# Holding four weight slots at each end of a product, with a ring of five raw and four high slots

## What is computed

```python
h = rmsnorm(x, g_pre_mix)
proj = h @ w_in                                   # 1024 x 3404: four attentions, 4 heads of 64 each
mix = concat(o_a, o_b, o_c, o_d)                  # sparse, forgetting, differential, sliding window
x = x + rmsnorm(mix @ w_out, g_post_mix)
h = rmsnorm(x, g_pre_mlp)
m = square(relu(h @ w_up)) @ w_down               # 4096 hidden
x = x + rmsnorm(m, g_post_mlp)
x = x + sigmoid(x @ w_ple_gate) * (p_i @ w_ple_proj)
```

## Time and profile before

| | |
|---|---|
| median of 3 runs | 2321.94 us (2321.07 to 2325.41) |
| the profiled execution: time | 2323.49 us |
| its span | 2321.5 us |
| mean granted TensorE clock | 0.942 |
| PE busy | 93% |
| DVE, ACT, POOL busy | 69%, 53%, 24% |
| read from HBM | 474 MB, 205 GB/s over the span |

### The profile page before, as it was taken

How to read it: one execution, slowest core, us unless ns; L and a number is a source line. 1 busy time by engine, 2 the same in 40 slices (tenths; PEclk the granted TensorE clock), 3 DMA queues, 4 the chain that set the end, 5 groups by cost and what they waited for, 6 DMA issues and landing times.

```text
span 2321.5 us, 28810 instructions
## 1 busy us (share of the span) xinstructions
PE 2150.0 (93%) x10728; PEld 1817.6 (78%) x10728; DVE 1600.0 (69%) x1615; ACT 1230.7 (53%) x1284; POOL 560.2 (24%) x355
## 2 busy tenths in 40 slices
PE   7978999898899989889998988799999999999995
PEld 5766888676778878777887877688888888888884
DVE  6675543577554358655345865698988989889896
ACT  4353443444454345443443544377777777777772
POOL 3413455332254533224554312000000000000000
PEclk9968999997799999899999989799999999999997
DMA  8403555442255544305554410499999999999993
GB/s 296 133 10 108 183 177 200 139 155 66 73 161 179 191 167 139 107 1 182 185 182 163 146 55 1 154 352 335 358 346 339 360 344 355 341 344 354 348 356 124
DMA packets 150508, 476.33 MB, mean 205 GB/s; under 512 B 12329, under 2 KB 39441, under 8 KB 150289
## 3 DMA queue, kind: packets, MB, share of 16 engines
q1 hardware_dynamic: 147792, 465.65, 56.9%
q0 software_dynamic: 2624, 9.44, 1.2%
HBM read 474.00 MB, written 1.05 MB: 205 GB/s over the span
## 4 chain that ended last, share of the span: by engine, by line
PE 78%; DVE 15%; ACT 3%; issue 2%; POOL 1%; DMA 0%; DVEq 0%; SPq 0%; POOLq 0%; ACTq 0%
PE G L581 19%; PE G L583 18%; PE G L582 18%; PE Sp L581 4%; PE Sp L583 4%; PE Sp L582 4%; PE G L607 3%; DVE ring_lo L1631 2%; PE Sp L744 2%; PE G L1136 1%; DVE ARENA L2074 1%; ACT ring_hi L1241 1%; PE G L1164 1%; PE G L1013 1%; PE Sp L1029 1%
## 5 line engine op out<-in xcount | busy, mean ns | idle before, releaser
L2307 DVE TENSOR_TENSOR e_lo<-e_raw,e_hi 128x1408 fp32r<-128x1408 f32 x384 | 600.8, 1619 | 27.0 <-ACT e_hi L1565 25.3
L1565 ACT ACTIVATE e_hi<-e_raw 128x1408 fp32r<-128x1408 f32 x384 | 520.7, 1380 | 159.1 <-DMA e_raw<-in_moe_w_down 55.9
L2407 POOL TENSOR_TENSOR ring_lo<-ring,ring_hi 128x640 fp32r<-128x640 f32 (+2 forms) x179 | 451.2, 2524 | 612.9 <-ACT ring_hi L1241 601.1
L1631 DVE TENSOR_TENSOR ring_lo<-ring,ring_hi 128x1408 fp32r<-128x1408 f32 (+2 forms) x179 | 320.6, 1799 | 292.1 <-ACT ring_hi L1241 291.0
L1241 ACT ACTIVATE ring_hi<-ring 128x2048 fp32r<-128x2048 f32 (+2 forms) x179 | 335.8, 1883 | 295.1 <-PE G L583 293.6
L581 PE MATMUL G<-ring_hi,xTh 128*128 128x512 f32 (+2 forms) x976 | 396.1, 406 | 36.6 <-DVE xTl L1647 30.6
L582 PE MATMUL G<-ring_lo,xTh 128*128 128x512 f32 (+2 forms) x976 | 387.3, 397 | 0.0
L583 PE MATMUL G<-ring_hi,xTl 128*128 128x512 f32 (+2 forms) x976 | 386.7, 396 | 0.0
L581 PE MATMUL G<-e_hi,xgTh 128*128 128x512 f32 (+1 forms) x768 | 290.0, 378 | 4.2 <-DVE e_lo L2307 4.2
L583 PE MATMUL G<-e_hi,xgTl 128*128 128x512 f32 (+1 forms) x768 | 289.1, 376 | 0.0
L582 PE MATMUL G<-e_lo,xgTh 128*128 128x512 f32 (+1 forms) x768 | 287.0, 374 | 0.0
(11 more groups left out here) (390 smaller groups left out, 3058.4 us busy)
## 6 DMA issues: line engine op xcount, KB each, us to landing
e_raw<-in_moe_w_gate SPq DMA_DIRECT2D x128, 704.0 KB, 5.9
e_raw<-in_moe_w_up SPq DMA_DIRECT2D x128, 704.0 KB, 5.9
e_raw<-in_moe_w_down SPq DMA_DIRECT2D x128, 704.0 KB, 5.9
ring<-in_w_in SPq DMA_DIRECT2D x48, 1024.0 KB, 5.1
ring<-in_w_mlp_up SPq DMA_DIRECT2D x32, 1024.0 KB, 5.3
ring<-in_w_mlp_down SPq DMA_DIRECT2D x32, 1024.0 KB, 4.8
ring<-in_w_out SPq DMA_DIRECT2D x16, 1024.0 KB, 4.9
ring<-in_ffn_w_gate SPq DMA_DIRECT2D x22, 512.0 KB, 3.8
```

Of the source, the lines that this page charges most:

```text
L1565: nc.scalar.activation(e_hi[:, u, :], e_raw[:, u, :], ACT.Copy).then_inc(w_hi.sem, 1)
L1631: v.tensor_tensor(ring_lo[:, n % R, cs], ring[:, n % R, cs], ring_hi[:, n % H, cs].bitcast(F32), ALU.subtract).then_inc(w_lo.sem, 1)
L2307: v.tensor_tensor(e_lo[:, u, :], e_raw[:, u, :], e_hi[:, u, :].bitcast(F32), ALU.subtract).then_inc(w_lo.sem, 1)
L2407: g.tensor_tensor(ring_lo[:, t % R, cs], ring[:, t % R, cs], ring_hi[:, t % H, cs].bitcast(F32), ALU.subtract).then_inc(w_lo_pool.sem, 1)
```

## The change

The ring becomes R = 5 raw and H = 4 high slots, in the same memory. Four slots are held at the end and at the start of products (`LEAD`): all of token block 0, then all of block 1.

- `product_rows` holds its last four slots. In block 1's last slot, after the first of its four groups, stands `tail()`: the transposes of block 0 for the next product.
- `lead` takes the place of `transposed_in`: block 0 through four slots, with the transposes of block 1 behind the first group of the fourth; then block 1 through four. Products over columns lead with two chunks (four slots, four banks), and wait for T0 and T1 and for their banks one by one. `product_tokens` is one lead with a tail. The first chunk of `w_in_2` keeps two slots (`first_chunk`).
- The low parts of 24 slots are made by DVE whole (`whole_dve`): the leading four of w_in in layer 1, of w_up twice, w_ple_proj and w_ple_gate twice (five each), and the first two of w_in_2.
- On ACT, DVE and POOL the parts of the next product's leading slots are put between the steps of the norms; before, only one stood ahead of them.

```diff
-R = 6
-H = 3
+R = 5
+H = 4
+LEAD = 4
...
+    whole_dve = []
     for l in range(DEPTH):
+        if l:
+            whole_dve += range(len(TILES), len(TILES) + LEAD)
         for n0, n1 in IN_CHUNKS:
             TILES += uses_cols(w["w_in"][l], n0, n1)
         TILES += uses_rows(w["w_out"][l])
+        whole_dve += range(len(TILES), len(TILES) + LEAD)
         for n0 in range(0, D_FF, 512):
             TILES += uses_cols(w["w_mlp_up"][l], n0, n0 + 512)
-        TILES += uses_rows(w["w_mlp_down"][l]) + uses_rows(w["w_ple_proj"][l]) + uses_rows(w["w_ple_gate"][l])
+        TILES += uses_rows(w["w_mlp_down"][l])
+        whole_dve += range(len(TILES), len(TILES) + 1 + LEAD)
+        TILES += uses_rows(w["w_ple_proj"][l]) + uses_rows(w["w_ple_gate"][l])
+    whole_dve += range(len(TILES), len(TILES) + 2)
...
-    def of_dve(m):
-
-        return m * 11 // 32 * 2
+    def of_dve(n):
+
+        m = floats_of(TILES[n])
+        return m if n in whole_dve else m * 11 // 32 * 2
+
+    def pool_parts(n):
+
+        return n - sum(t < n for t in whole_dve)
...
-            pe.wait_ge(w_lo_pool.sem, n + 1)
+            pe.wait_ge(w_lo_pool.sem, pool_parts(n + 1))
...
-        def transposed_in(src, ready, part, banks, between=None):
-
-
-            token_transposes(src, 0, ready)
-            if between:
-                between()
+        def lead(src, ready, part, banks_of, slots_per_half, tail, after_first=None):
+
+            slots = []
+            for j in range(LEAD):
+                if j == 0:
+                    bank_free_t(0)
+                if j == slots_per_half:
+                    bank_free_t(1)
+                banks_free(banks_of(j, 0))
+                slots.append(weights())
+                if j == LEAD - 1:
+                    part(slots[j], j, 0, range(1))
+                    token_transposes(src, 1, ready)
+                    last = part(slots[j], j, 0, range(1, 4))
+                else:
+                    last = part(slots[j], j, 0, range(4))
+                if j == 0 and after_first:
+                    after_first()
+            if slots_per_half == 2:
+                last.then_inc(g_half.sem, 1)
+            for j in range(LEAD):
+                if j == 0:
+                    bank_free_t(0)
+                if j == slots_per_half:
+                    bank_free_t(1)
+                banks_free(banks_of(j, 1))
+                if j == LEAD - 1 and tail:
+                    part(slots[j], j, 1, range(1))
+                    tail()
+                    last = part(slots[j], j, 1, range(1, 4))
+                else:
+                    last = part(slots[j], j, 1, range(4))
+                last.then_inc(w_used.sem, 1)
...
+        def first_cols(src, ready, widths, by):
+
+            lead(src, ready, lambda slots, j, tb, groups: cols_tile(slots, j % 2, tb, widths[j // 2], 2 * (j // 2) + tb, groups),
+                 lambda j, tb: [2 * (j // 2) + tb], 1, None)
+            for q in range(2):
+                chunk_made([2 * q, 2 * q + 1], by)
+
...
+        def product_rows(ah, al, n_tiles, by, behind, tail):
+
+
+            banks_free(range(4))
+            for t in range(n_tiles - LEAD):
...
-                for j in range(2):
+                for j in range(LEAD):
+                    k0 = 2 * (n_tiles - LEAD + j)
                     if tb == 0:
                         slots.append(weights())
-                    last = rows_tile(slots[j], 2, ah, al, 2 * (n_tiles - 2 + j), 2 * n_tiles, tb, g_of(tb))
+                    elif j == LEAD - 1:
+                        rows_tile(slots[j], 2, ah, al, k0, 2 * n_tiles, tb, g_of(tb), range(1))
+                        tail()
+                    last = rows_tile(slots[j], 2, ah, al, k0, 2 * n_tiles, tb, g_of(tb), range(1 if tb and j == LEAD - 1 else 0, 4))
                     if tb:
                         last.then_inc(w_used.sem, 1)
-                    elif j:
+                    elif j == LEAD - 1:
                         last.then_inc(g_half.sem, 1)
-            chunk_made(range(4), by, times)
-
-        def product_tokens(src, ready, by, between=None, times=1):
-
-            transposed_in(src, ready, lambda slots, j, tb: rows_tile(slots, 2, xTh, xTl, 2 * j, KT, tb, g_of(tb)), range(4), between)
-            product_rows(xTh, xTl, KT // 2, by, 2, times)
+            tokens_made(by)
...
+        def product_tokens(src, ready, by, tail, after_first=None):
+
+            lead(src, ready, lambda slots, j, tb, groups: rows_tile(slots, 2, xTh, xTl, 2 * j, KT, tb, g_of(tb), groups),
+                 lambda j, tb: [2 * tb, 2 * tb + 1], 2, tail, after_first)
+            tokens_made(by)
...
-            product_tokens(XN, o_block, ("dve",))
+            token_transposes(XN, 0, o_block)
+            product_tokens(XN, o_block, ("dve",), lambda: token_transposes(XN, 0, xn_block))
...
-            product_rows(hTh, hTl, 16, ("dve",), behind=(lambda: hidden(7), own_embedding))
+            product_rows(hTh, hTl, 16, ("dve",), (lambda: hidden(7), own_embedding), lambda: token_transposes(X, 0, x_block))
...
-            product_tokens(X, x_block, ("act",), embed_second, NTB)
+            product_tokens(X, x_block, ("act",), lambda: token_transposes(XN, 0, xn_block) if l + 1 < DEPTH else token_transposes(X, 0, x_block), embed_second)
...
-            first_cols(X, x_block, IN2_CHUNKS[0][1] - IN2_CHUNKS[0][0], [0, 1], ("act",))
+            first_chunk(X, x_block, IN2_CHUNKS[0][1] - IN2_CHUNKS[0][0], ("act",))
...
-            product_tokens(XN, xn_block, ("dve",))
+            token_transposes(XN, 0, xn_block)
+            product_tokens(XN, xn_block, ("dve",), lambda: token_transposes(X, 0, x_block))
...
         def normed_in(n, of_product):
 
 
-            met(n, 1)
+            met(n, 0)
             for tb in range(NTB):
                 of_product(tb)
-                if tb:
-                    block_evac(0)
+                met(0, 1 + 2 * tb)
                 mean_square_of_x(tb)
-            met(0)
-            block_evac(1)
+                met(0, 2 + 2 * tb)
+                block_evac(tb)
...
-            met(15, 1)
-            for tb in range(NTB):
-                mean_square_of_product(tb)
-            met(0)
-
-            met(1)
-            for tb in range(NTB):
-                if tb == 0:
-                    act.wait_ge(pe2a.sem, pe2a.next("act"))
-                else:
-                    act.wait_ge(w_used.sem, n_use["act"])
-                nc.scalar.activation(PLR[:, tb, :], Sp[:, :, :].rearrange("p b n -> p (b n)"), ACT.Copy).then_inc((a2d if tb else a2pe).sem, 1)
-                block_evac(tb)
+            met(15, 0)
+            mean_square_of_product(0)
+            met(0, 2)
+            block_evac(0)
+            met(0, 3)
+            mean_square_of_product(1)
+            act.wait_ge(pe2a.sem, pe2a.next("act"))
+            nc.scalar.activation(PLR[:, 0, :], Sp[:, :, :].rearrange("p b n -> p (b n)"), ACT.Copy).then_inc(a2pe.sem, 1)
+            met(1, 3)
+            act.wait_ge(w_used.sem, n_use["act"])
+            nc.scalar.activation(PLR[:, 1, :], Sp[:, :, :].rearrange("p b n -> p (b n)"), ACT.Copy).then_inc(a2d.sem, 1)
+            met(0, 4)
+            block_evac(1)
...
         def normed_in(n, addend, gain):
 
-            met(n, 1)
+            met(n, 0)
             g_half.next("dve")
             for tb in range(NTB):
                 addend(tb)
-                if tb:
-                    block_evac(0)
                 added_to_x(tb, d2a)
+                met(0, 1 + 2 * tb)
                 pre_norm(tb, gain)
-            met(0)
-            block_evac(1)
+                met(0, 2 + 2 * tb)
+                block_evac(tb)
...
-            met(15, 1)
+            met(15, 0)
             g_half.next("dve")
-            for tb in range(NTB):
-                normed_product(tb, VEC[:, 0, :])
-                added_to_x(tb, d2pe)
-
-            met(1)
-            token_evac()
+            normed_product(0, VEC[:, 0, :])
+            added_to_x(0, d2pe)
+            met(0, 2)
+            block_evac(0)
+            met(0, 3)
+            normed_product(1, VEC[:, 0, :])
+            added_to_x(1, d2pe)
+            met(1, 4)
+            block_evac(1)
...
             for tb in range(NTB):
                 residual(tb)
-                if tb and s is d2pe:
-                    block_evac(0)
                 moments(XN, tb, D, s_out)
                 scaled(tb)
+                if tb == 0 and s is d2pe:
+                    met(0, 1)
+                    block_evac(0)
+                    met(0, 2)
...
-            met(4, 1)
+            met(4, 0)
             post_norm(g_tokens, block_sum, X, d2pe)
             vec_free.append(d2pe.made)
-            met(0)
+            met(0, LEAD)
             if l == 0:
...
-        def layer_norm(s_in=d2p, s_out=p2d):
+        def layer_norm(s_in=d2p, s_out=p2d, between=None):
             for tb in range(NTB):
                 pool.wait_ge(s_in.sem, s_in.next("pool"))
```

(12 more changed lines are left out.)

165 lines of the change are left out of this document (88 added, 77 removed).

## The result

The changed kernel takes **2287.72 us** (median of 4 runs, 2283.83 to 2287.91) beside 2323.68 (4 runs) for the kernel before on the same chip: ratio 0.9836, 95% interval 0.9811 to 0.9862, 36 us faster. My 2281 us is 0.9824 of the time it was made against. The profiled execution after is 2287.86 us, its span 2285.9.

The account below looks back on a forecast made before the run. PE, busy 93% of the span, bounds the kernel; gains lie in its waits and clock. 39.3 + 2.0 + 2.4 - 2.5 = 41.2 off 2323.5 gives 2282.3, stated as 2281 us; range 2265 to 2302.

Parts of the forecast that it names:

- the eight places: Places between products, from w_out to w_up through feed-forward to w_in_2: 67.2 us lost before, 27.9 after, 39.3 gained.
- the clock elsewhere: Three places keeping waits of 0.6 to 1.1 us: 1.0 us each lost to the clock, 3.0 in all.
- The transposes without a wait: w_out to w_up: block 0's XN ends 8.55 us after g_half, its transposes are wanted at 8.9, so none wait.
- four low parts in time at w_down: w_down to gate: all four low parts in time, the last by 0.1 us; loss 0.5 us, twice.
- The tight steps: w_out to w_up: PE waits 1.05 us for xTl, third low part 0.55 late, fourth 1.1 late; loss 2.7.
- w_out_2 to the feed-forward: Third leading slot ready at 22.5 us, wanted at 17.3: 5.2 us of waiting plus 2.4 of clock, 7.6.
- The feed-forward: Feed-forward to w_in_2 of layer 1: PE waits 5.5 us for block 1's X, plus 2.4 of clock, 7.9.
- DVE's rotation: w_in: first chunk finishes later and DVE's rotation moves with it, costing 1.5 us in layer 0, 1.0 in layer 1.
- The router and the early starts: Router's block 1 layer norm starts earlier, gain 2.0 us; four products start without xTl's second half, gain 2.4.
- The rival of half the gain: PE waits for DVE: every hold between products keeps 2.5 us more, eight cost 20, 2301 us; chance 0.17.
- the one of blocking transposes: Inside block 1's last slot, transposes stall PE if block 0's XN is 1.5 us late: 12 us, 2293; chance 0.14.
- The wait on loads that would have made it slower: Loads over three slots, 16.3 us, would stall ACT with chunk evacuations behind it: 2370 us; chance 0.03.

Follow-up runs that it names:

- the control: The changed kernel run again as it is, in another set of runs: 2281.62 us, 0.9809 of the kernel before.
- experiment 2: Changed kernel with every low part shared by DVE and POOL, POOL's behind each block's second root: 2285.49 us, 0.9854.
- experiment 3: Changed kernel with block 0's transposes for the next product behind the last held slot instead of inside it: 2288.63 us, 0.9848.
- experiment 6: Changed kernel with DVE's evacuation of block 0 (xTl) ahead of the second leading slot's low part: 2288.77 us, 0.9849.
- experiment 5: Changed kernel with the layer norms' leading low parts whole on DVE and the last ones ahead of block 1's standardizing row: 2275.86 us, 0.9807.
- experiment 10: Changed kernel with the layer norms' leading low parts made whole by DVE but left in their place: 2282.66 us, 0.9809.
- experiment 11: Changed kernel with low parts still shared, DVE's last ones at the layer norms moved ahead of block 1's standardizing row: 2279.23 us, 0.9788.
- experiment 12: Changed kernel with experiment 5's edit, feed-forward's second part behind the norm, and two slots leading layer 0's w_in with parts behind block 1's evacuation: 2275.05 us, 0.9776.
- experiment 4: Changed kernel with only two slots leading the first input product of layer 0: 2285.97 us, 0.9833.
- experiment 1: Kernel before with five raw and four high slots and nothing else changed: 2336.74 us, 1.0059.

## Why the prediction was right, and where it was off

**What bounds.** Right: the gain came at the eight places, from waits and from the clock behind them. In the windows of the earlier trace rows 87 matmuls ran at half pace before, at the same places 23 after: at 0.2 us each, 13 us of the gain are the clock's. The waits left and the half-paced matmuls (0.2 us each): w_out to w_up 3.2 in both layers; w_down to gate none; gate to w_in 2.3 (0.60 and 1.67); gate to w_in_2 1.5; w_out_2 10.8 (7.97 and fourteen matmuls); feed-forward 8.3 (6.52 and nine). **29.3 us, against 24.9 of my sum without its term for the clock elsewhere, 27.9 with it.** That the control's 45 us lie above my 41 is luck: the stretches of the change gave 36 to 38, and the attention and mixing stretches the rest.

**The transposes without a wait, four low parts in time at w_down.** Right; there PE waits for nothing where I gave 0.5. The clock in windows over the first six places was 1.00 (I gave 0.9 or more), over the last two 0.81.

**The tight steps.** Their sum was right to half a us (2.7 forecast, 3.2 measured), their shares not: xTl 0.8 for 1.05, the third part 0.7 for 0.55, the fourth 1.65 for 1.1. The root was later than I had it: beside DVE's whole part POOL's first row took 1.25 us instead of 0.22 (207.75), so XN resumed at g_half + 7.9, not + 7.0. Experiments 2, 3 and 6 show that no single step sets the place: shared parts, later transposes and another order gave 3.5 (and seven half-paced matmuls), 3.7 and 3.7 us of waits.

**w_out_2 to the feed-forward, the step that failed most.** I took 5.2 us for the third slot's wait and measured 7.97. My chain had the norm's rows at their undisturbed length and put POOL's blocking outside the sum, up to 3 us. The rows above show it in full: L2077 took 2.57 and 2.44 us instead of 1.23, L2067 1.94 instead of 0.81, 3.7 us in all, each beside a part of POOL. The Trainium skill's exclusive lock (SBUF — State Buffer, Who interferes with whom) is what these rows show, in both directions: 2.57 for 1.23 on DVE, and 2.32 for 0.23 on POOL in experiment 5. By that rule the sum at this place would have been nearly right, 5.2 and up to 3 for 7.97. But experiment 10 shows that taking POOL out leaves 6.74 us of the wait, since DVE then works 2.7 us more; experiment 11 shows that the place of the last two parts is what counts. The blocked time was only in part to be won back.

**The feed-forward.** 5.5 forecast, 6.52 measured. Two rows of DVE were blocked there too (2.57 us for 1.23, 1.94 for 0.81), but experiment 10, with only the second of them blocked, waited 6.96; so the blocking alone is not shown to be the cause. Half pace nine matmuls, not twelve.

**The clock elsewhere.** I took 3.0 us for the places with waits of 0.6 to 1.1 us; none of them, nor those of 1.5 to 1.7, was followed by a matmul at half pace. Where I didn't look, in the attention units, the time moved by 6.6 us between two executions of the same kernel, one of them with the low clock throughout.

**DVE's rotation.** The mechanism was right and the size off in layer 0: 1.5 forecast, 3.1 measured. The wait that I had named grew by 1.4 us (3.49 to 4.92), as forecast; beside it stand terms that I had at nothing, a new wait of 0.62 us for DVE (AT_, at 66.8) and ten half-paced matmuls at the start for six (0.8 us). In layer 1 it was 1.0 against 1.3 (PE's wait 3.37 against 2.07). Experiment 12 shows by undoing it that the leading slots cost the 3.1 us; experiment 4 alone would have misled, by its time and by its stretch.

**The router and the early starts.** -2.7 us in the stretch where I gave -2.6, but 0.6 of mine was for the early start, which falls ahead of the stretch's first matmul; so 2.7 stand against 2.0. The mechanism was right (block 1's residual starts 25.5 us into the stretch, 26.8 before, and xTl is no longer in its way), and experiment 3 shows what it hangs on: with the transposes behind the slot the 2.6 us are lost again. PE's waits at the four early starts sum to 5.2 us for 7.8, a gain of 2.6 for 2.4.

**The rivals.** The rival of half the gain did not come true, nor did the one of blocking transposes; between most products the transposes could even stand later. The wait on loads that would have made it slower did not show: landing is 5.2 to 5.8 us at w_out to w_up, and 7.2 at most from 200 to 1300 us. What I had called free, a fourth high slot and one raw slot fewer in the unchanged order, costs 0.6% (experiment 1), and the change pays for it by placing every part.

**Still open.** Why the units get some full clock in most executions and 0.50 throughout in others. Whether experiment 12 beats experiment 5 (2275.05 and 2275.86 us in different sets) can't be told from these runs; that it beats the changed kernel rests on its stretches (-3.0 us at the start, -3.5 at the layer norms beside the control) more than on the medians.

## What to carry to other kernels

Between two products, list the engine that works without a gap and the order of its queue: moving the parts that hold up the next product ahead of the norm's rows won 4 to 6 us here (experiment 11), while sharing such work with a second engine that blocks the first cost some 5 (experiment 2). A constant such as a ring's depth can be an order in disguise: every `ahead` that follows it makes one part more at each place. Undo a suspected cost on all engines that follow it. Read the experiment by the stretch it touches, since the clock elsewhere moves the whole by more than such an edit, and check the clock inside the stretch too: a median that shows no difference hid 5 us in experiment 2.
